# A two-block transformer forward pass on one core: the half products of two feed-forward layers and the selector's dots get fewer, wider matmuls

## The reference

```python
def swiglu(xn, w_gate, w_up, w_down):
    return (jax.nn.silu(xn @ w_gate) * (xn @ w_up)) @ w_down
# selector, per block of 128 queries
rel = jax.nn.relu(jnp.einsum("bqhd,bsd->bqhs", iq_b, ik))
score = jnp.einsum("bqh,bqhs->bqs", iw_b, rel)
```

## Time and profile before

| | us |
|---|---|
| median of three timed runs | 2120.97 |
| the profiled execution, whole | 2124.32 |
| its span, first to last instruction | 2122.5 |
| TensorE busy | 2100.3 (99%) |
| VectorE / ScalarE / Pool busy | 1490.9 / 1099.6 / 566.4 |
| windows of s0st, s1st, s2st | 1236.9 to 1278.3, 1301.5 to 1382.1, 1439 to 1499.7 |

### The profile page before, as it was taken

How to read it: one execution, slowest core, us unless ns; L and a number is a source line. 1 busy time by engine, 2 the same in 40 slices (tenths; PEclk the granted TensorE clock), 3 DMA queues, 4 the chain that set the end, 5 groups by cost and what they waited for, 6 DMA issues and landing times.

```text
span 2122.5 us, 32375 instructions
## 1 busy us (share of the span) xinstructions
PE 2100.3 (99%) x12084; PEld 1826.0 (86%) x12084; DVE 1490.9 (70%) x2424; ACT 1099.6 (52%) x1925; POOL 566.4 (27%) x476
## 2 busy tenths in 40 slices
PE   9999999999999999999999999999999999999998
PEld 6887898888888889888887899999887778999897
DVE  7778334677567687776777687878656885868775
ACT  5877433435444344353776354554445763544543
POOL 2100431242333120153674331201222222311012
PEclk9999999999999999999999999999999999999999
DMA  8887212445676565634845569987562235555663
GB/s 260 252 261 207 84 59 70 149 160 202 236 208 178 146 190 179 156 112 139 281 176 169 141 192 251 275 256 224 156 166 86 77 91 158 169 185 183 208 188 130
DMA packets 148348, 372.01 MB, mean 175 GB/s; under 512 B 39008, under 2 KB 43360, under 8 KB 132832
## 3 DMA queue, kind: packets, MB, share of 16 engines
q1 hardware_dynamic: 129600, 241.49, 34.0%
q0 software_dynamic: 10448, 76.55, 17.2%
q10 hardware_dynamic: 8144, 51.91, 6.9%
HBM read 356.78 MB, written 132.64 MB: 231 GB/s over the span
## 4 chain that ended last, share of the span: by engine, by line
PE 87%; DVE 6%; ACT 2%; DMA 2%; issue 1%; DVEq 1%; POOLq 0%; POOL 0%; SPq 0%; ACTq 0%
PE bank L430 8%; PE bank L431 8%; PE bank L434 8%; PE bank L552 6%; PE bank L555 6%; PE bank L553 6%; PE bank L998 5%; PE bank L1002 5%; PE bank L1000 5%; PE bank L448 4%; PE bank L447 4%; PE bank L449 4%; PE bank L2537 2%; PE bank L1798 1%; DVE b_wl L355 1%
## 5 line engine op out<-in xcount | busy, mean ns | idle before, releaser
L344 ACT ACTIVATE b_wh<-b_raw 128x1024 fp32r<-128x1024 f32 (+1 forms) x312 | 321.8, 1034 | 547.7 <-PE bank L434 241.7
L355 DVE TENSOR_TENSOR b_wl<-b_raw,b_wh 128x1024 fp32r<-128x1024 f32 (+2 forms) x269 | 339.2, 1263 | 124.6 <-ACT b_wh L344 120.3
L552 PE MATMUL bank<-b_xh,b_wh 128*128 128x512 f32 x712 | 294.9, 414 | 0.6 <-DVE b_wl L355 0.4
L553 PE MATMUL bank<-b_xl,b_wh 128*128 128x512 f32 x712 | 278.5, 391 | 0.0
L555 PE MATMUL bank<-b_xh,b_wl 128*128 128x512 f32 x704 | 276.3, 393 | 0.0
L1206 POOL TENSOR_TENSOR b_yl<-b_arena,b_yh 128x512 fp32r<-128x512 f32 x42 | 67.6, 1610 | 536.6 <-ACT b_yh L1117 344.3
L430 PE MATMUL bank<-b_xh,b_wh 128*128 128x512 f32 x504 | 196.9, 391 | 0.0
L431 PE MATMUL bank<-b_xl,b_wh 128*128 128x512 f32 x504 | 196.2, 389 | 0.0
L434 PE MATMUL bank<-b_xh,b_wl 128*128 128x512 f32 x496 | 193.1, 389 | 0.0
L355 POOL TENSOR_TENSOR b_wl<-b_raw,b_wh 128x1024 fp32r<-128x1024 f32 (+1 forms) x45 | 104.0, 2310 | 228.9 <-ACT b_wh L344 191.2
L555 PEld LDWEIGHTS bank<-b_xh,b_wl 128*128 128x128 f32 x704 | 132.3, 188 | 29.2
(11 more groups left out here) (579 smaller groups left out, 5550.4 us busy)
## 6 DMA issues: line engine op xcount, KB each, us to landing
scr_sums<-in_quarters POOLq DMA_DIRECT2D x37, 1024.0 KB, 9.3
scr_sums<-in_quarters ACTq DMA_DIRECT2D x35, 1024.0 KB, 5.3
b_raw<-scr_sums SPq DMA_DIRECT2D x110, 256.0 KB, 3.4
b_more_raw<-scr_sums SPq DMA_DIRECT2D x108, 256.0 KB, 3.4
scr_sums<-scr_sums POOLq DMA_DIRECT2D x24, 1024.0 KB, 8.6
b_raw<-in_quarters SPq DMA_DIRECT2D x92, 256.0 KB, 3.1
b_more_raw<-in_quarters SPq DMA_DIRECT2D x76, 256.0 KB, 3.0
scr_sums<-in_quarters ACTq DMA_DIRECT2D x8, 1536.0 KB, 9.3
```

The lines of the kernel that those rows point to most:

```text
L344: act.activation(panel_hi_lo(n)[0][:, cols], raw_of(n)[:, cols], ACT.Copy).then_inc(w_hi, 1)
L355: dve.tensor_tensor(lo, raw_of(n)[:, cols], hi.bitcast(F32), ALU.subtract).then_inc(w_lo, 1)
L552: pe.matmul(bank[:, :], ph[:, w], hi[:, x, :], start=(k == 0), stop=False)
L553: last = pe.matmul(bank[:, :], ph[:, w], lo[:, x, :], start=False, stop=(n in SIDE_BY_SIDE and k == kt - 1))
```

## The change

In the half products the high and the low part of the input become one moving operand of 512 columns. For each slice, two matmuls stand where three stood: weights' high part x (high | low), 512 columns into a whole bank, and weights' low part x high, 256 columns into the half of the bank that holds the high part's result. The value is then the sum of a bank's two halves. VectorE's five subtractions and ScalarE's two copies out of the banks work on 512 columns, and Pool adds the two halves where a result leaves the scheme (`fold_halves`: four additions of 128x256 per pair, for both halves of the value and of the gate). ScalarE applies Silu once, to the folded 512 columns, and after it VectorE's `gated` runs at the next pair's product 1, no longer at product 0. `down_sum` of s1st and m1st moves from VectorE to Pool, with a drain before each of its three operations, ahead of the low part of the same pair. ScalarE copies product 4 into `p1` too, once VectorE has read the copy of product 0 there. The arena grows by 512 columns.

In the selector a head's query tile holds its high part in its own 64 rows and its low part in the other 64. The keys' high part stands in all 128 rows, so one matmul gives high x high + low x high, and a second one, with the keys' low part, the rest: two matmuls per dot. The copies and subtractions that make the query tiles are done by halves of the rows; one Pool fill of zeros goes.

```diff
+        xs_both = [operands(f"seven{i}", arena_at + 4 * min(20 + 2 * i, at) * T, xs_apart[i] + 1, 2 * T) for i, at in enumerate(xs_at)]
+        xs_hi, xs_lo = ([x[:, xs_apart[i] * ((20 + 2 * i > xs_at[i]) == is_hi), :].rearrange("p (k t) -> p k t", k=4)
+                         for i, x in enumerate(xs_both)] for is_hi in (True, False))
-        gt, vt, p1 = sg, cv, take(38 * T, T // 2)
+        gt, vt, p1 = sg, cv, take(21888, T)
...
+        def both_parts(i, k):
+
+            return (xs_both[i][:, 0:xs_apart[i] + 1:xs_apart[i], k * (T // 2):(k + 1) * (T // 2)],
+                    slice(0, T // 2) if 20 + 2 * i < xs_at[i] else slice(T // 2, T))
+
         def differences(ch):
-            return (cg[:, 0:T // 2], cg[:, T // 2:T]) if ch else (first_tmp, first_un)
+            return (ssq[:, :], cg, rrow[:, :]) if ch else (ssq[:, :], take(36 * T, T), take(39 * T, T))
+
+        def folded(ap):
+            return ap[:, 0:T // 2], ap[:, T // 2:T]
...
-                bank = pb[SEVEN_BANK[i]][:, 0:T // 2]
+                bank = pb[SEVEN_BANK[i]]
                 ph, pl = panel_hi_lo(n)
                 for k in range(4):
                     w = slice(half * T + k * P, half * T + k * P + P)
-                    pe.matmul(bank, ph[:, w], xs_hi[i][:, k, :], start=(i < 4 and k == 0), stop=False,
-                              skip_group_check=(i > 3))
-                    pe.matmul(bank, ph[:, w], xs_lo[i][:, k, :], start=False, stop=False,
-                              skip_group_check=(i > 3))
-                    m = pe.matmul(bank, pl[:, w], xs_hi[i][:, k, :], start=False, stop=(k == 3),
-                                  skip_group_check=(i > 3))
+                    x_both, hi_part = both_parts(i, k)
+                    pe.matmul(bank[:, :].rearrange("p (a t) -> p a t", a=2), ph[:, w], x_both, start=(i < 4 and k == 0),
+                              stop=False, skip_group_check=True)
+                    m = pe.matmul(bank[:, hi_part], pl[:, w], xs_hi[i][:, k, :], start=False, stop=(k == 3),
+                                  skip_group_check=True)
                 m.then_inc(mm_done if half else even_done, 1)
         def seven_dve(dve, seg):
             ch, q0, pairs, before = SEVEN[seg]
             hidden0 = HIDDEN_BEFORE[seg[0]] + PAIRS[ch][0] + q0
-            tmp, un = differences(ch)
+            tmp, un, v0 = differences(ch)
             def quarter(i):
-                return pb[SEVEN_BANK[i]][:, 0:T // 2]
+                return pb[SEVEN_BANK[i]][:, :]
             def gated(q):
+                dve.wait_ge(value_folded, folded0 + 2 * (before + q) + 2)
                 dve.wait_ge(gate_silu, hidden0 + q + 1)
                 if ch > 0:
                     wait(dve, y_ready, YR[seg[0]] + PAIRS[ch][0] + q0 + q)
...
             for j in range(7 * pairs):
                 n, q, i = BASE[seg] + j // 2, j // 7, j % 7
                 p = before + q
-                if i == 0 and q > 0:
-                    gated(q - 1)
                 if i in (1, 2, 3, 5, 6):
                     product_done(dve, seg, j)
                 if i == 1:
                     dve.wait_ge(p1_copied, p1_0 + p + 1)
                     dve.tensor_tensor(un, quarter(1), p1, ALU.subtract).then_inc(out_free, 3 + p % 2)
+                    if q > 0:
+                        gated(q - 1)
                     dve.drain()
                 if i == 2:
+                    wait(dve, gate1_folded, p, folded0)
                     dve.tensor_tensor(tmp, quarter(2), un, ALU.subtract).then_inc(quarter_read, 1)
                     dve.drain()
                 if i == 3:
-                    dve.tensor_tensor(vt[:, T // 2:T], quarter(3), tmp, ALU.add).then_inc(quarter_read, 1)
+                    dve.tensor_tensor(vt, quarter(3), tmp, ALU.add).then_inc(quarter_read, 1)
                 if i == 5:
-                    dve.tensor_tensor(vt[:, 0:T // 2], quarter(5), un, ALU.subtract).then_inc(quarter_read, 1)
+                    dve.tensor_tensor(v0, quarter(5), un, ALU.subtract).then_inc(quarter_read, 1)
                 if i == 6:
                     dve.tensor_tensor(tmp, quarter(6), un, ALU.subtract).then_inc(quarter_read, 1)
                     dve.drain()
...
-                if ch == 1 and q > 0 and i in (2, 4, 5):
-                    down_sum(dve, seg[0], q - 1, (2, 4, 5).index(i))
...
             gated(pairs - 1)
             if n - 2 in DOWN_OF:
                 split_lo(dve, n + 1, 0, (n + 1) % 2, KT_OF[n + 1])
-            if ch == 1:
-                down_sum(dve, seg[0], 7, 0)
-                down_sum(dve, seg[0], 7, 1)
-                down_sum(dve, seg[0], 7, 2).then_inc(sums_lo, 1)
-
-        def down_sum(dve, l, q, part):
-            dve.drain()
+
+        def down_sum(eng, l, q, part):
+            eng.drain()
             x0, x1 = product_of(l, 0, q)[:, T0], product_of(l, 0, q)[:, T1]
             if part == 0:
-                return dve.tensor_tensor(x1, x1, product_of(l, 1, q)[:, T1], ALU.subtract)
+                return eng.tensor_tensor(x1, x1, product_of(l, 1, q)[:, T1], ALU.subtract)
             if part == 1:
-                return dve.tensor_tensor(x0, x0, x1, ALU.subtract)
-            return dve.tensor_tensor(DOWN_TILES[l].third[:, q, :], product_of(l, 1, q)[:, T0], x0, ALU.subtract)
+                return eng.tensor_tensor(x0, x0, x1, ALU.subtract)
+            return eng.tensor_tensor(DOWN_TILES[l].third[:, q, :], product_of(l, 1, q)[:, T0], x0, ALU.subtract)
+
+        def fold_halves(pool, l, ch, q):
+
+            seg = f"{l}{ch}st"
+            _, q0, _, before = SEVEN[seg]
+            p, (tmp, _, v0) = before + q - q0, differences(ch)
+            pool.wait_ge(quarter_read, 4 * p + 2)
+            pool.tensor_tensor(vt[:, T // 2:T], *folded(vt), ALU.add).then_inc(value_folded, 1)
+            pool.wait_ge(gate0_read, p + 1)
+            pool.wait_ge(prod_done, HIDDEN_BEFORE[l] + PAIRS[ch][0] + q - (ch == 0 and q == q0))
+            if ch == 2 and q == 0:
+                pool.wait_ge(out_free, BASE[seg])
+            pool.tensor_tensor(gt[:, 0:T // 2], *folded(p1), ALU.add).then_inc(gate0_folded, 1)
+            pool.wait_ge(quarter_read, 4 * p + 3)
+            pool.wait_ge(value_folded, folded0 + 2 * p + 1)
+            pool.tensor_tensor(vt[:, 0:T // 2], *folded(v0), ALU.add).then_inc(value_folded, 1)
+            pool.wait_ge(quarter_read, 4 * p + 4)
+            pool.tensor_tensor(gt[:, T // 2:T], *folded(tmp), ALU.add).then_inc(gate1_folded, 1)
         def add_down(dve, l, i):
             b, part, tiles = i % 2, i // 2, DOWN_TILES[l]
...
-            tmp, _ = differences(ch)
-
-            def gate1(q):
-                act.wait_ge(quarter_read, 4 * (before + q) + 4)
-                act.activation(gt[:, T // 2:T], tmp, ACT.Silu).then_inc(gate_silu, 1)
+
+            def gates(q):
+                act.wait_ge(gate0_folded, folded0 + before + q + 1)
+                act.wait_ge(gate1_folded, folded0 + before + q + 1)
+                act.activation(gt, gt, ACT.Silu).then_inc(gate_silu, 1)
             def product_hi(q):
                 act.wait_ge(prod_done, hidden0 + q + 1)
...
                 if i == 0:
+                    product_done(act, seg, j)
+                    wait(act, gate0_folded, before + q, folded0)
+                    act.activation(p1, pb[SEVEN_BANK[0]][:, :], ACT.Copy).then_inc(p1_copied, 1)
                     if q > 0:
-                        gate1(q - 1)
-                    product_done(act, seg, j)
-                    act.activation(p1, pb[SEVEN_BANK[0]][:, 0:T // 2], ACT.Copy).then_inc(p1_copied, 1)
-                if i == 1 and q > 0:
+                        gates(q - 1)
+                if i == 2 and q > 0:
                     product_hi(q - 1)
...
-                    act.wait_ge(prod_done, hidden0 + q - (ch == 0 and q == 0))
-                    if ch == 2 and q == 0:
-                        act.wait_ge(out_free, BASE[seg])
-                    act.activation(gt[:, 0:T // 2], pb[SEVEN_BANK[4]][:, 0:T // 2], ACT.Silu).then_inc(gate0_read, 1)
+                    act.wait_ge(quarter_read, 4 * (before + q) + 1)
+                    act.activation(p1, pb[SEVEN_BANK[4]][:, :], ACT.Copy).then_inc(gate0_read, 1)
             n = BASE[seg] + CNT[seg] + 2
             if n - 2 in DOWN_OF:
                 split_hi(act, n, 0, n % 2, KT_OF[n])
-            gate1(pairs - 1)
+            gates(pairs - 1)
...
                     beside[q]()
+                if l != "c":
+                    fold_halves(pool, l, ch, q)
+                    if ch == 1:
+                        pool.wait_ge(prod_done, HIDDEN_BEFORE[l] + first + q + 1)
+                        down_sum(pool, l, q, 0)
+                        down_sum(pool, l, q, 1)
+                        last = down_sum(pool, l, q, 2)
+                        if q == 7:
+                            last.then_inc(sums_lo, 1)
...
```

(32 more changed lines are left out.)

23 lines of the change are left out of this document (11 added, 12 removed).

## The result

The changed kernel takes 2173.4 us (median of four runs, 2170.9 to 2176.5) against 2121.2 for the kernel before beside it: ratio 1.0243, interval 1.0231 to 1.0255. It is 52 us slower. The forecast was 2132 with a range up to 2149; the direction was right, the size was not, and the range did not hold the time.

The account below looks back on a forecast made before the run. TensorE, busy 99%, was taken as the bound, with Pool's circle overtaking it in s1st and m1st. Terms -4.2 (dots) - 1.2 + 14.0 + 1.8 + 1.0 = +11.4 us on 2120.97 gave 2132 us, range 2112 to 2149.

Parts of the forecast that it names:

- Part 1: Half-product matmuls on TensorE: a slice falls from 360 to 354 ns (347 to 361), 6 us over 36 pairs.
- Part 2: Selector: 24 dots lose their third matmul, 4.2 us less; extra copies and subtractions cost 0, at most 1 us.
- Part 4: Pool's added folds and down_sums, called the deciding term: +14.0 us over s1st and m1st, +7.0 each.
- the circle: s1st, m1st: gated product, down_sums, low part, folds, Silu, next gated product; 8.3 us alone, 11.3 with three splits.
- s0st and m0st: Stages without down_sum: a turn of 10.0 us with 3 splits, about TensorE's own; -0.6 us each.
- m2st: Stage where TensorE sets the pace (-1.0), but four turns of h bring it to +0.1 us.
- s2dn: At its start the folds delay the last low part that TensorE needs: +1.0 us.
- Everything collides: Rival: turns of 12.0 us in s1st and m1st, 10.5 in s0st and m0st; 2146 us, chance 0.17.
- the first rival: Pool keeps up, its turn stays below 9.9 us and TensorE sets everything: 2110 us (2103 to 2117), chance 0.18.

Follow-up runs that it names:

- splits_from_bank: sum_by_signal with VectorE's weight splits of s1st, s2st, m1st, m2st reading an unused PSUM bank in place of the raw weights: 2135.1 us, ratio 1.0061.
- sum_by_signal: The changed kernel with Pool's drains in down_sum replaced by waits for a semaphore that the step before raises: 2159.1 us, ratio 1.017.
- folds_first: sum_by_signal with Pool's first two folds of the first pair of s0st and m0st ahead of its three steps for the last ordinary pair: 2155.2 us.
- narrow folds: sum_by_signal with the four folds of a pair done on 16 of 256 columns, all waits as they are: 2125.8 us, ratio 1.0016.
- own_copy: sum_by_signal with ScalarE copying product 4 to a buffer of its own in s0st, m0st, m1st and m2st: 2159.0 us, ratio 1.0174.

## Why the prediction was wrong

- **Bound, and the order of reading it.** Right: TensorE was the bound, and it began to stand in s1st and m1st at VectorE's reads of the banks.
- **Part 1, matmuls.** Right: 353 ns a slice for a forecast of 354, 6.5 us for 6. The operand across two tiles costs nothing.
- **Part 2, dots.** Right: 3.9 us in the profile for 4.2.
- **Part 4, the circle, in m1st.** Right in mechanism and nearly in size: forecast 11.3 us a turn and 87.6 for the stage; 11.56 and 90.6. That splits count was borne out by splits_from_bank. Their number was set low: the forecast let 3 of 3.5 fall into the circle, and by turns 3 and 4 did. The 87.9 of sum_by_signal is no second proof of the 87.6, which had three drain gaps of 0.15 us a turn in it, while sum_by_signal has none. Of the 2.7 us between 87.9 and 90.6 up to 1.5 are the clock, the rest drains.
- **The step that failed most: part 4 in s1st.** The prediction took the circle of s1st for that of m1st: +7.0 for each, where +21.6 and +10.0 were measured. It priced a drain at 0.15 us, from the earlier trace rows, where no DMA stood ahead; and it left `add_sum` out of the circle, though it is Pool's and stands in s1st. Drain and DMA together cost 12.6 us, up to 3.4 of them through TensorE's clock, a third of the 36 by which the span missed. Both halves were in the trace of before (the DMA issues on Pool, landing after 9 us), but no row showed a drain behind one. The prediction had no second price for a drain that waits for a DMA, though the landing times to take it from were there to be read.
- **s0st and m0st.** Wrong: -0.6 forecast, +5.6 and +5.0 measured. The prediction reckoned the steady turn (10.0 us against 9.9) and not the entry, where Pool's folds stand behind a wait for the last ordinary pair. That order costs 1.0 us where no half-clock stretch follows, 1.9 where one does (folds_first); the folds' length is part of the rest, and some 2.4 us of each stage stay open.
- **m2st** +2.7 for +0.1, and s0dn, s1dn and m1dn +5.3, for which the sum had no term. It had one, +1.0, for s2dn, where the profile has +0.2. That the last folds, Silu and gated product of a stage are late for the down projection is argued; s0dn goes back to 23.0 us with narrow folds, and nothing more was taken apart.
- **Rivals.** None had it. "Everything collides" (2146) was the nearest and was built from the same turn with more splits; what was wanted was a second mechanism in the circle, not a longer first one.
- **The direction** was right, with 11 us forecast and 52 measured. Two small slips in the sums had no part in that: 347 ns a slice is 9.72 us a pair, not 9.70, and the first rival's -6.6 for the matmuls is -6.1 by the forecast's own 9.91.

## What to carry to other kernels

Before work is put on an engine, list what that engine's queue already holds in that stage, DMA issues above all, and price each new drain or wait behind the longest of them. A chain that closes on itself has to be shorter than the bound by all that can delay it; drains of 10 us cost nothing beside it, and shorter ones 12.6 us in it. Two idle engines that exclude each other are not two free engines: price an operation by what will run beside it. And the largest wait in the list need not be the cause: taking it away (own_copy) changed nothing.
